# First layer of a two-layer encoder trunk: memory tokens brought in by columns, start-up loads and splits in another order, sums over x by narrow matmuls

## What is computed

```python
h = rmsnorm(x, p['norm_in'][i])
z = h @ p['a_w_in'][j]                      # b_w_in in the second layer
...
def memory_attention(q, mem, mem_norm, w_mem_kv, q_norm, k_norm):
    q = rmsnorm(q.reshape(B, S, MEM_HEADS, MEM_HEAD_DIM), q_norm)
    kv = rmsnorm(mem, mem_norm) @ w_mem_kv
    k = rmsnorm(kv[..., :MEM_WIDTH].reshape(B, N_MEM, MEM_HEADS, MEM_HEAD_DIM), k_norm)
    v = kv[..., MEM_WIDTH:].reshape(B, N_MEM, MEM_HEADS, MEM_HEAD_DIM)
```

## Time and profile before

| what | value |
|---|---|
| median of 3 runs | 1362.87 us (1362.62 to 1364.82) |
| the profiled execution, its own time | 1364.05 us |
| its span in the profile | 1362.2 us |
| TensorE busy | 1345.4 us (99% of the span) |
| VectorE, ScalarE, GpSimd busy | 887.6, 679.8 and 403.5 us |
| first matmul of `memV` starts at | 12.08 us |
| first matmul of `qmem` starts at | 36.85 us |

### The profile page before, as it was taken

One profiled execution on the slowest core, in us unless ns is written; L12 is line 12 of the kernel. 1 busy time (PEld: TensorE's weight loads), 2 busy tenths in 40 slices (PEclk: granted clock), 3 DMA queues, 4 the chain that ended last, 5 costly groups with the idle time before them and its releaser, 6 DMA issues.

```text
span 1362.2 us, 20507 instructions
## 1 busy us (share of the span) xinstructions
PE 1345.4 (99%) x7173; PEld 1167.5 (86%) x7173; DVE 887.6 (65%) x1793; ACT 679.8 (50%) x1547; POOL 403.5 (30%) x519
## 2 busy tenths in 40 slices
PE   8999999999999999999999999999999999999999
PEld 6889988888888889888788898888888888898887
DVE  7756688887785657888673523767766634266871
ACT  6554466555564536777551422555454323167660
POOL 1221252331012323746202212423300122337560
PEclk9999999999999999999999999999999999999999
DMA  7867753343778486634776545323144652654225
GB/s 239 321 233 265 249 190 135 134 165 110 266 227 291 149 303 233 235 106 149 265 265 217 195 138 189 113 89 98 51 163 147 198 179 81 215 182 154 91 74 185
DMA packets 109334, 248.20 MB, mean 182 GB/s; under 512 B 11056, under 2 KB 48816, under 8 KB 109232
## 3 DMA queue, kind: packets, MB, share of 16 engines
q1 hardware_dynamic: 103760, 239.19, 51.8%
q10 hardware_dynamic: 5472, 7.69, 1.8%
HBM read 158.76 MB, written 88.08 MB: 181 GB/s over the span
## 4 chain that ended last, share of the span: by engine, by line
PE 90%; DVE 5%; ACT 3%; DMA 1%; issue 1%; POOL 0%; ACTq 0%; SPq 0%; DVEq 0%
PE bank L1847 25%; PE bank L1849 25%; PE bank L1848 25%; PE bank L1892 7%; PE bank L1853 2%; PE bank L1854 2%; PE bank L2207 2%; ACT prob L780 1%; DVE w_split L1141 1%; DVE probT L1148 1%; DVE prob L1589 1%; DMA w_raw<-in_w_mem 0%; ACT o_low L1083 0%; DVE xs L1254 0%; DMA w_split<-kept_w 0%
## 5 line engine op out<-in xcount | busy, mean ns | idle before, releaser
L1847 PE MATMUL bank<-actT,w_split 128*128 128x512 f32 x544 | 214.9, 395 | 0.0
L1849 PE MATMUL bank<-actT,w_split 128*128 128x512 f32 x544 | 212.2, 390 | 0.0
L1723 POOL TENSOR_TENSOR prob<-prob,rinv 128x256 f32<-128x256 f32 x192 | 132.7, 722 | 253.2 <-DVE rinv L1272 253.2
L1141 DVE TENSOR_TENSOR w_split<-w_raw,w_split 128x512 fp32r<-128x512 f32 (+3 forms) x212 | 150.4, 724 | 86.1 <-ACT w_split L747 82.0
L747 ACT ACTIVATE w_split<-w_raw 128x512 fp32r<-128x512 f32 (+3 forms) x212 | 126.4, 607 | 127.6 <-PE bank L1849 53.6
L1847 PE MATMUL bank<-w_split,actT 128*128 128x512 f32 (+3 forms) x512 | 170.8, 334 | 0.5 <-DVE w_split L1141 0.3
L1848 PE MATMUL bank<-w_split,actT 128*128 128x512 f32 (+3 forms) x512 | 170.2, 332 | 0.0
L1849 PE MATMUL bank<-w_split,actT 128*128 128x512 f32 (+3 forms) x512 | 170.2, 332 | 0.0
L1848 PE MATMUL bank<-actT,w_split 128*128 128x512 f32 x384 | 149.9, 390 | 0.0
L762 ACT ACTIVATE sq<-bank 128x512 f32<-128x512 f32 (+4 forms) x128 | 60.6, 480 | 136.1 <-PE bank L1849 129.7
L1160 DVE TENSOR_REDUCE ss<-sq 128x2 f32<-128x384 f32 (+5 forms) x120 | 63.3, 541 | 95.7 <-ACT sq L762 95.0
(11 more groups left out here) (185 smaller groups left out, 3127.8 us busy)
## 6 DMA issues: line engine op xcount, KB each, us to landing
kept_w<-w_split SPq DMA_DIRECT2D x112, 512.0 KB, 5.0
w_split<-kept_w SPq DMA_DIRECT2D x112, 512.0 KB, 3.6
w_raw<-in_w_mem SPq DMA_DIRECT2D x64, 256.0 KB, 3.8
w_raw<-in_w_out SPq DMA_DIRECT2D x48, 256.0 KB, 3.7
kept_w<-part_split SPq DMA_DIRECT2D x24, 512.0 KB, 4.1
w_raw<-in_w_b SPq DMA_DIRECT2D x48, 256.0 KB, 4.2
part_split<-kept_w SPq DMA_DIRECT2D x24, 512.0 KB, 4.1
w_raw<-in_w_a SPq DMA_DIRECT2D x32, 256.0 KB, 3.9
```

Of the source, the lines that this page charges most:

```text
L1141: dve.tensor_tensor(halves(n)[1], w_raw[:, RAW_AT[n] % RAW, 0:width], halves(n)[0].bitcast(fp32), ALU.subtract).then_inc(w_lo_dve, 1)
L1723: pool.tensor_tensor(t, t, rinv[:, par, i:i + 1].to_broadcast(list(t.shape)), ALU.mult).then_inc(p_pool, 1)
L1847: nc.tensor.matmul(out, lhs[0], rhs[0], start=start, stop=False, skip_group_check=skip)
L1849: return nc.tensor.matmul(out, lhs[1], rhs[0], start=False, stop=stop, skip_group_check=skip)
```

## The change

It alters pass 0 before `qmem`, and one piece of every pass. The memory is loaded by columns in pass 0 too (four transfers of 256 KB) and split from there like in later passes. The rows are loaded later, into a free place, and are read by ScalarE alone, for the sums of squares. The scale of each token goes on `memV` as it leaves its bank, which is moved between the first x tiles. SP's loads and the splits on ScalarE and VectorE get new orders. The first `across` of pass 0 becomes eight narrow matmuls with the halves as the stationary operand and two columns of ones as the moving one, after tile 2 of `memK` in place of tile 0. In every pass the scaled identity is made by VectorE, directly as two halves, and GpSimd keeps one power. There are 10 matmuls on constants in place of 13.

```diff
-FIRST_WEIGHTS = (1, 1, 2, 2, 3, 4, 4, 4)
-X_WEIGHTS = (1, 2, 3, 4, 4, 4, 5, 6)
+X_AHEAD_OF = (5, 7, 8, 10, 12)
+X_SUM_AT = 2
+FIRST_SCALE_AT = 5
+FIRST_COLUMNS = (1, 1, 2, 2, 4, 4, 4, 4)
+FIRST_SQUARES = (5, 7, 7, 8, 8, 10, 10, 11)
+X_WEIGHTS = ((2, 2, 3, 4, 5, 5, 6, 7), (1, 2, 3, 4, 4, 4, 5, 6))
...
-        if L == 0:
-            take([("memT", L, j) for j in range(KD // 2)])
...
+        if L == 0:
+            for j in range(NM):
+                free[uses["memV", L, j][0]] = clock[0] + j
...
@@ SyncE
+                load_weights(0, 1)
+                load_columns(0, 0)
+                load_weights(1, 2)
+                load_columns(0, 1)
+                load_weights(2, RAW)
+                load_columns(0, 2)
+                load_columns(0, 3)
+                load_weights(RAW, X_AHEAD_OF[0])
+                for i in range(NT):
+                    load_x(0, i)
+                    load_weights(X_AHEAD_OF[i], X_AHEAD_OF[i + 1])
                 for j in range(NM):
-                    sp.dma_start(mem_in[:, j, :], mem[0, j * P:(j + 1) * P, :]).then_inc(mem_loaded[j], 16)
...
+                    sp.dma_start(last_rows[:, NM + j, :], mem[0, j * P:(j + 1) * P, :]).then_inc(mem_loaded[j], 16)
+                    load_weights(X_AHEAD_OF[NT] + j, X_AHEAD_OF[NT] + j + 1)
+                load_weights(X_AHEAD_OF[NT] + NM, FIRST["qmem", 0, NT - 1])
@@ ScalarE
+                def first_columns():
+                    w_hi_to(FIRST["memV", 0, NM - 1] + 1)
+                    act.wait_ge(first_in, 32)
+                    for k in range(KD):
+                        a = GAIN_AT["mem0"] + k
+                        w_hi_to(FIRST["memV", 0, NM - 1] + FIRST_COLUMNS[k])
+                        act.wait_ge(mem_cols_loaded[k // 2], 16)
+                        act.activation(memT[:, 0, k, :], mem_cols_in[:, k, :], ACT.Copy, scale=gcol[:, a:a + 1]).then_inc(hi_done, 1)
+                    w_hi_to(FIRST["memV", 0, NM - 1] + FIRST_SQUARES[0])
...
-                for dst, src in ((ident[:], ident_in), (gcol[:], gains)):
+                for dst, src in ((gcol[:], gains), (ident[:], ident_in)):
...
                         for f in range(KD):
                             x_square(L, f)
-                            w_hi_to(v_at + SPLIT + FIRST_WEIGHTS[f])
+                            w_hi_to(v_at + FIRST_SQUARES[f])
...
+                    if L == 0:
+                        w_hi_to(k_at + X_SCALE_AT + 1)
+                        first_squares()
                     w_hi_to(k_at + X_SCALE_AT + 4)
                     if L == 0:
                         act.wait_ge(warm_done, 1)
+                        w_hi_to(q_at + 2)
...
+                        if L == 0 and k < NM:
+                            mem_values(range(k, k + 1))
@@ VectorE
+                def x_scale_halves(L):
...
+                    dve.wait_ge(rrx_ready, L + 1)
+                    link(dve.tensor_copy(rr_hi[:], rr_x[:]))
+                    link(dve.tensor_tensor(rr_lo[:], rr_x[:], rr_hi[:].bitcast(fp32), ALU.subtract))
+                    dve.tensor_tensor(tokens_of(0), eye, over_tokens(rr_hi), ALU.mult)
+                    dve.tensor_tensor(tokens_of(1), eye, over_tokens(rr_lo), ALU.mult).then_inc(norm_split, 1)
...
+                def first_columns():
+                    for k in range(KD):
+                        w_lo_to(FIRST["memV", 0, NM - 1] + FIRST_COLUMNS[k])
+                        memory_low(0, k)
+                    w_lo_to(FIRST["memV", 0, NM - 1] + FIRST_SQUARES[0])
...
                         for f in range(1, KD):
-                            w_lo_to(v_at + SPLIT + FIRST_WEIGHTS[f - 1])
                             x_add(L, f)
+                            w_lo_to(v_at + FIRST_SQUARES[f])
@@ GpSimd
-                    rsqrt(ss_x[:], rr_x[:], NT, D, rrx_ready)
-                    pool.wait_ge(rrx_ready, L + 1)
-                    pool.tensor_tensor(x_slots[:, 0, :].rearrange("p (t n) -> p t n", t=NT), ident[:].unsqueeze(1).to_broadcast([P, NT, P]),
-                                       rr_x[:].unsqueeze(2).to_broadcast([P, NT, P]), ALU.mult).then_inc(diag_ready, 1)
+                    pool.tensor_tensor(rr_x[:], ss_x[:], mhalf[:, 0:NT], ALU.pow).then_inc(rrx_ready, 1)
@@ TensorE
-                warm(11)
+                warm(9)
                 pe.wait_ge(first_in, 32)
-                warm(2).then_inc(warm_done, 1)
+                warm(1).then_inc(warm_done, 1)
...
+                        for t in range(NT):
+                            for a in range(2):
+                                ins = nc.tensor.matmul(bank(use)[:, 2 * t:2 * t + 2], norm_halves[:, a, t * P:(t + 1) * P],
+                                                       ones[:, 0:2], start=a == 0, stop=a == 1, skip_group_check=True)
...
-                    mem_chunk("memK", {X_SCALE_AT: x_scales} if L > 0 else {0: x_sums, 5: x_scales})
+                    mem_chunk("memK", {X_SCALE_AT: x_scales} if L > 0 else {X_SUM_AT: token_sums, FIRST_SCALE_AT: x_scales})
```

More of the change, by code:

```diff
@@ L448, in trunk_kernel @@
         rr_x, _ = place("rr_x", [P, NT], fp32)
+        rr_hi, _ = place("rr_hi", [P, NT], fp32r)
+        rr_lo, _ = place("rr_lo", [P, NT], fp32r)
         ss_kr, _ = place("ss_kr", [P, NT], fp32)
@@ L1211, in token_sums @@
                     dve.wait_ge(*full(use))
+                    if L == 0:
+                        sums = bank(use)[:, 0:2 * NT].rearrange("p (t c) -> p t c", c=2)[:, :, 0]
+                        dve.tensor_scalar(ss_x[:], sums, 1.0 / D, EPS, ALU.mult, ALU.add).then_inc(read(use)[0], 1)
+                        dve.wait_ge(*read(use))
+                        dve.sem_inc(ssx_ready, 1)
+                        return
                     dve.tensor_tensor(v, bank(use)[:].rearrange("p (t n) -> p t n", t=NT),
@@ L1351, in _ @@
                                                  op1=ALU.subtract).then_inc(x_split, 1)
[L1352 removed]
+                        if L == 0 and k == 0:
+                            mem_values(range(1))
+                            x_scaled_tile(L, 1)
+                            w_lo_to(q_at + 2)
+                        elif L == 0 and k == 1:
+                            x_scaled_tile(L, 2)
+                            mem_values(range(1, NM))
+                        w_lo_to(q_at + X_WEIGHTS[L > 0][k])
                     norm([("memK", L, j) for j in range(NM)], MW, MH,
                          lambda use: bank(use)[:].rearrange("p (h d) -> p h d", h=MH),
[L1355 removed]
+                         lambda j: k_mem_st[:, j, :].rearrange("p (h d) -> p h d", h=MH), FIRST["qmem", L, NT - 1] + KD - 1)
                     w_lo_to(FIRST["gate", L, 11] + SPLIT)
@@ L1920, in fill @@
                             ins.then_inc(used[TILES[tile][7]], 1)
-                def memory_rows():
-                    for j in range(KD // 2):
-                        pe.wait_ge(*vacant(("memT", 0, j)))
-                    for i in range(NM):
-                        pe.wait_ge(xn_ready, count("xn"))
-                        for k in range(KD):
-                            use = ("memT", 0, k // 2)
-                            c = (k % 2) * NMEM + i * P
-                            ins = nc.tensor.transpose(bank(use)[:, c:c + P], xn[i][:, k * P:(k + 1) * P], ident[:])
-                            if i == NM - 1 and k % 2 == 1:
-                                ins.then_inc(full(use)[0], 1)
                 def warm(n):
```

144 lines of the change are left out of this document (60 added, 84 removed).

## The result

The changed kernel takes 1368.16 us in the median of 11 runs (1365.07 to 1369.66), the kernel before 1363.20 (11 runs, 1362.15 to 1364.82). The ratio is 1.0033, with a 95% interval of 1.0025 to 1.0040: slower by over 0.2%. The profiled execution took 1368.49 us, with a span of 1366.7, 4.5 more than before. In 9 of the 11 runs the mean granted clock is 0.998 or 0.999 (median 1368.25 us); the two at 1.00 took 1365.07 and 1366.43, still more than the kernel before.

The account below looks back on a forecast made before the run. TensorE, busy 99%, bounds the kernel, so the start of `qmem` decides: 32.3 against 36.85 us takes 4.5 off 1364.05, giving 1359.5, or 1358.4 against the median. Forecast 1358.5 us, range 1356.0 to 1361.6.

Parts of the forecast that it names:

- First product: Start of pass 0: TensorE's first useful matmul at 6.65 us against 12.08, with ends 6.0 and 7.7.
- Narrow matmuls: Pass 0, eight matmuls replacing the first `across`: taken at 1.1 us, with ends 0.45 and 1.8.
- The chain of the scales: Pass 0, leading to the second `across`: 3.0 us against 5.5 before, fitting the 4.1 us between tiles 2 and 5.
- Clock at the first products: Start of pass 0: the clock no longer falls to 0.50 at 12 us, saving 1.5 us.
- Supply: Loads up to tile 8, first of `memK`: ready at 19.0 us, wanted at 17.5; 1.5 us given back, bounds 0 and 3.
- Tile 16: First weight tile of `qmem`: issued at about 26 us behind five table loads, landing at 29.5 or 30.
- the gap: TensorE's stall just before `qmem`: 0.8 us in place of 0.4.
- The tables hold tile 16: Rival before `qmem`: SP held 2.6 us or tile 16 landing late; `qmem` at 34.5 to 35.2, 1360.5 to 1361.2 us; chance 0.18.
- its second form: Alternative within the tables rival, before `qmem`: tile 16 lands after 6 us; chance 0.18 for the whole rival.
- DMA-bound because the memory is loaded twice: Rival at the splits of tiles 12 and 13: at 175 GB/s `qmem` starts at 39.9, 1365.9 us; chance 0.05.
- Later passes: Passes after pass 0, new scale chain: costed at nothing; without cover 0.7 us in each of three passes.

Follow-up runs that it names:

- e1: The changed kernel with the five table loads issued after the eight `qmem` weight tiles instead of before them: median 1362.28 us, ratio 0.9989 to the kernel before.
- e9: e1 without the loads of the memory's rows, ScalarE squaring the column buffer instead: one execution, 1362.44 us.
- e7: e1 with the memory's columns in two loads of 512 KB instead of four of 256 KB: 1362.84 us, ratio 1.0004 to the kernel before.
- e2: The changed kernel with both halves of the first x written before the waits for weight tiles 16 and 17: 1365.41 us, ratio 1.0013 to the kernel before.
- e3: The changed kernel with sixteen matmuls on data at hand put into TensorE's gap before `qmem`: 1366.82 us, ratio 1.0027 to the kernel before.
- e4: The kernel before with the five table loads moved behind the eight `qmem` weight tiles: 1363.45 us, ratio 0.9996 to the unedited kernel before.

## Why the prediction was wrong

It gave 1358.5 us, 1356.0 to 1361.6, faster with a chance of 0.72. It was wrong in its sign. Point by point:

- **First product.** "6.65", measured 7.08, within its ends. The gains had `first_in` at 5.5 in place of 5.2.
- **Narrow matmuls.** "I take 1.1", measured 0.80 from start to start (0.95 by their row). The chain of the scales, taken at 3.0 us, lasts from 27.44, the end of the narrow matmuls, to 31.07, the end of the last half, 3.6 us, and fits into its three tiles.
- **Clock at the first products.** It stayed, as forecast. But "1.5 us are saved" was read from one profiled execution that had the fall, and 19 of 33 executions don't have it, as far as their mean clock tells. The sum did set that execution against the median, and took off the 1.2 us between them; it did not ask what they were made of.
- **Supply.** "1.5 us of the gain go back here", measured 4.3. Two reasons. The start moved 239 GB/s and not the 322 that I took from the kernel before. By the stretches the 4.98 MB for tile 8 are in at 17.5 us (4.19 MB at 15.2, then 340 GB/s) and not at 15.2 to 16.1. Second, I priced the wait ahead of tile 8 alone. Tiles 2 and 5 waited too (0.92 and 0.84), and tile 10 waited 1.26 for the last quarter of x, which landed at 22.2 and has squares, additions and a split behind it.
- **Tile 16.** This is the step that failed most: "In the new order tile 15 goes out after the split of tile 11, at about 23.3. Five table loads of 0.5 bring tile 16 to about 26 and its landing to 29.5 or 30." VectorE's split of tile 11 stands behind the halves of the sums, and so behind that same quarter of x: it ended at 26.4. The tables went out at 26.80, hardly before the old 26.9, tile 16 at 29.18, and it landed 6.8 us later, at 36.0. I priced the gap at 0.8 and it is 4.0. Even with no table ahead of it tile 16 goes out at 28.44 (e1), when VectorE has split tile 12, so the issue at 26 was out of reach for a second reason.
- **What I had as a rival.** "The tables hold tile 16", with 0.18, was the right mechanism, in its second form (a late landing; SP itself was not held). It said 34.5 to 35.2, since it held SP or the landing at what the kernel before showed and kept the issue at 26. What happened is both: a later issue and a landing above the longest of the weights'. I had not priced the clock's fall in such a gap, 1.8 us.
- **DMA-bound because the memory is loaded twice**, the only rival on the slower side, is not what happened: e9 takes the second load away, and TensorE waits the same. For the sign it was the wrong mechanism, and the right one was not followed to its end.
- **Later passes.** Costed at nothing, and in e1 they cost nothing: 1359.9 - 34.64 = 1325.3 us from `qmem` to the end, as before. But the cover is thin. In seven of eleven traces TensorE waits for the new chain there, 0.3 to 1.3 us, and this was not followed up.

From my `qmem` at 32.3 to the 38.86 measured: first product 0.4, supply 2.8, narrow matmuls -0.3, gap 3.4, sum 6.3 of 6.6. To the time of the profiled execution the second fall of the clock adds 1.8, the rest of the program 0.7, and the 1.2 that I had taken off for the other fall. With the tables out of the way (e1) the change is worth 1.2 us against the kernel before with the same edit (medians of 1362.28 and 1363.45, from the same set of runs; no interval was made for the pair). That agrees with `qmem` at 34.64 against 35.52, both at the full clock: 5 us won at the first product, and four given back to the supply.

What stays open: why loads with 2 KB for each partition move 240 GB/s at the start and those of 4 KB 292; why e7's earlier `qmem` doesn't reach the time; what makes the new chain late in the later passes of some executions; and what in the broadcast loads keeps the engines idle.

## What to carry to other kernels

When a front part is made faster, look for holds that it covers: list what the queue issues between the last covered load and the first uncovered one, and ask when each lands, not only when it is issued. Small loads that nobody needs soon belong behind the loads that the bottleneck waits for, in a place where the hold that goes with them is covered. And before a fall of the clock is counted as a gain, look at how many executions have it, and price the clock in every gap that the change may open.

## What the runs showed of the hardware

- Three broadcast loads of 72 KB in all, 256 and 64 bytes for each of 128 partitions, hold back what the queue has behind them: 23 GB/s at a busy share of 0.09 for 3 us, where the same stretch without them moves 191 at 0.61, and a 256 KB load lands after 6.8 us in place of 2.8. In e2 and e3, with the same order of loads, it is 79 and 25 GB/s and 6.2 and 5.6 us, and the hold goes where the loads go (94 GB/s from 45 to 50 us in e4). The Trainium skill, "DMA: Bandwidth & Descriptors", Specifications, says that transfers under 512 bytes miss the line rate. The trace agrees in direction, but the engines stand idle rather than work slowly, so that rule alone doesn't give the size.
- The same kernel has a mean clock under 1.00 in 14 of 33 executions and is 1.7 us slower in them; one such trace has the fall from 12 to 15.2 us. A gap of 4.00 us at 35 to 39 us brought a stretch of 3.4 us at 1.2 GHz, worth 1.8 us, and with sixteen matmuls in the gap the clock is 1.00 in 8 of 10 runs, where it was so in 2 of 11.
- The first 5 us of loads moved 220 to 242 GB/s in loads of 256 KB with 2 KB for each partition, 271 and 292 when the columns had 4 KB, and 322 in the kernel before.
- Eight matmuls of 128 x 2 with 128 columns of weights take 0.95 us by their row and 0.80 from start to start, 0.10 each, under half of a full matmul's 0.23.
